# Score products of an attention block: three passes over both groups, or two passes for each group on stacked query halves

## The chip, the cores and the metric

The kernel runs on one core of a Trainium2 chip. The metric is the device time of one execution in microseconds. Its engines are TensorE (PE in the profile, PEld for its weight loads), VectorE (DVE), ScalarE (ACT), GpSimd (POOL) and SyncE (SP), which issues the DMAs. They run side by side and wait for one another through semaphores.

## What is computed

One layer of a hybrid decoder on 1024 new positions (the prompt) and 8 single decode steps: an input projection, sliding-window attention and a gated linear recurrence side by side, an output projection, and a gated feed-forward layer, all in fp32. The change touches the attention of the prompt alone:

```
s = einsum('bnqhgd,bnkhd->bnhgqk', qb, kk) * HEAD_DIM ** -0.5   # window 128, 2 key/value heads
p = sink softmax over the masked s
o = einsum('bnhgqk,bnkhd->bqhgd' by block, p, vv)
```

There are 8 query heads of 64 dimensions and 2 key/value heads (groups). A block is 128 queries; it sees 256 keys, its own block and the one before (the first block sees 128).

## The kernel before

**Precision.** A product of fp32 matrices is made on TensorE from operands of the type fp32r. Each operand is split in a high part (a copy rounded to fp32r) and a low part (the difference), and three products are summed: high with high, high with low, low with high.

**Layout.** Activations lie with features on the 128 partitions. A query tile `mix[:, t]` holds head t of group 0 on partitions 0 to 63 and head t of group 1 on partitions 64 to 127. The keys `kraw` lie in the same way. The tiles `k_hi` and `k_lo` (128 x 2 x 1032) have a section for each group: in section g only the partitions of group g hold keys, the others are zero (memsets of POOL, lines 972 to 975). So one product with 128 partitions and both sections as moving operand (512 columns) gives the scores of both groups, and the zeros keep the groups apart.

**Order of the work.** The input projection is cut into units: 22 weight tiles by three chunks of 344 columns, 24 products each (line 1482, called by line 1529). A list ORDER gives their order; a unit has two ticks of 12 products. Every other step is hung on a tick, and each engine walks the ticks in order. The first four weight tiles (keys, values, the recurrence's input, query tile 0) run chunk by chunk, while the input's third chunk is still being loaded and split.

**Key steps.** When the keys' unit of chunk c is done and rotated (function `rope`, lines 1929 to 1933), ScalarE makes the high part of each group (lines 1174 to 1177) and VectorE the low part (`keys_low`, lines 1935 to 1941), which signals `k_low`. On VectorE's queue then follow the read of the next unit (line 1970), the reciprocal and diagonal tiles `diag` of the row norms (line 1882), for which TensorE waits at line 1513, and at chunk 1 the low part of the input's third chunk (line 1871), for which TensorE waits at line 1482.

**Attention items.** An item is one query tile and one block: 4 x 8 = 32 items, the first at tick 16, one every two ticks. Its steps are Q (ScalarE copies the queries' high part `q_hi`, line 1198; VectorE subtracts for `q_lo`, line 2044), S (TensorE's scores, lines 1557 to 1559; VectorE adds the mask and takes the maxima, line 2051; ScalarE's exponentials, line 1204), PT (transposes of the probabilities, line 1566), PV (product with the values, line 1575; scaling, line 2066) and OT (transpose back, line 1580). TensorE waits in S for `k_low`, for `q_low` of the item and for the maxima of the item before. From tick 54 on the recurrence runs beside it: for each of 4 heads a preparation on VectorE (lines 2076, 2077), a product of diagonals (line 1596) and seven levels (TensorE line 1611, VectorE lines 2013, 2014 and 2099). The loop over items ends before the second half of the recurrence; output projection and feed-forward (lines 1753, 1793) follow.

In the profile both `q_hi` and weight tiles copied by ScalarE carry line 1068, that of the helper `copy`.

Of the kernel before, what the change touches and what calls it, by code (L numbers as in the profile page):

```python
# [14 lines left out]
P = 128  # L15
# [191 lines left out]
def build(nc, t_in, t_out):  # L207
# [99 lines left out]
    q_hi, oo = at("q_hi", [P, 2, P], F32R, at_mix + 5 * 4 * ROWS)  # L307
    q_lo, _ = at("q_lo", [P, 2, P], F32R, oo)
# [386 lines left out]

    V_GROUPS = [(0, 4), (4, 4), (8, 1)]
# [272 lines left out]
    def _(pool):  # L969
        pool.memset(cos[:], 1.0).then_inc(sem("pool_set"), 1)  # L970
        pool.memset(sin[:], 0.0).then_inc(sem("pool_set"), 1)
        pool.memset(k_hi[:].bitcast(F32), 0.0).then_inc(sem("pool_set"), 1)
# [93 lines left out]
    def _(act):  # L1066
# [86 lines left out]
        for tick in range(TICKS):  # L1153
# [14 lines left out]
            for step in rot_steps(tick):  # L1168
                if step[0] == "k_high":
                    c = step[1]  # L1170
                    act.wait_ge(sem("rope"), ROPE_UNITS.index(unit_index("k", 0, c)) + 1)
                    if c == 0:
                        act.wait_ge(sem("pool_set"), 3)
                    for g in range(NKV):
                        h = slice(HD * g, HD * g + HD)
                        ins = copy(k_hi[h, g, cols(c)], kraw[h, cols(c)])
                    ins.then_inc(sem("k_high"), 1)
# [12 lines left out]
            for step, i in attention_steps(tick):  # L1190
                t, j, e = i // NBLK, i % NBLK, i % 2
                k0 = WIN if j == 0 else 0
                if step == "Q":
# [4 lines left out]
                    copy(q_hi[:, e, :], mix[:, t, P * j:P * j + P]).then_inc(sem("q_high"), 1)  # L1198
# [19 lines left out]
            for step in recurrence_steps(tick):  # L1218
                h = step[1]
                if step[0] in ("ita", "itb"):  # L1220
# [4 lines left out]
                    if h == 0 and not a:  # L1225
                        act.wait_ge(sem("pool_set"), 4 + CH)
# [248 lines left out]
    def _(pe):  # L1475
# [42 lines left out]
        for tick in range(TICKS):  # L1518
# [28 lines left out]
            for step, i in attention_steps(tick):  # L1547
                t, j, e = i // NBLK, i % NBLK, i % 2
                kbs = (1,) if j == 0 else (0, 1)
                if step == "S":  # L1550
# [6 lines left out]
                    for n, (a, b) in enumerate(((q_hi, k_hi), (q_hi, k_lo), (q_lo, k_hi))):  # L1557
                        mm = pe.matmul(out[:, :, k0:], a[:, e, :], b[:, :, P * (j - 1) + k0:P * (j + 1)], start=(n == 0), stop=(n == 2))
# [292 lines left out]
    def _(dve):  # L1851
# [83 lines left out]
        def keys_low(c):  # L1935
            dve.wait_ge(sem("k_high"), c + 1)
            dve.wait_ge(sem("pool_set"), 4 + c)
            for g in range(NKV):
                h = slice(HD * g, HD * g + HD)
                ins = dve.tensor_tensor(k_lo[h, g, cols(c)], kraw[h, cols(c)], k_hi[h, g, cols(c)].bitcast(F32), ALU.subtract)  # L1940
            ins.then_inc(sem("k_low"), 1)
# [82 lines left out]
        for tick in range(TICKS):  # L2024
# [14 lines left out]
            for step, i in attention_steps(tick):  # L2039
                t, j, e = i // NBLK, i % NBLK, i % 2  # L2040
                k0 = WIN if j == 0 else 0
                if step == "Q":
                    dve.wait_ge(sem("q_high"), i + 1)
                    dve.tensor_tensor(q_lo[:, e, :], mix[:, t, P * j:P * j + P], q_hi[:, e, :].bitcast(F32), ALU.subtract)\
                        .then_inc(sem("q_low"), 1)
# [24 lines left out]
            for step in recurrence_steps(tick):  # L2070
# [18 lines left out]
                if step[0] == "level":  # L2089
                    n = step[2]  # L2090
                    dve.wait_ge(sem("level_mm"), LEVELS * h + n + 1)
                    if n == 0 and h == 0:
                        dve.wait_ge(sem("pool_set"), 4 + CH)
# [38 lines left out]
            for step in sample_steps(tick):  # L2132
                n = DECB * NQ
                if step[0] == "ks_t":

                    dve.wait_ge(sem("pool_set"), 5 + CH)
# [426 lines left out]
```

## Time and profile before

| | |
|---|---|
| median of 3 runs | 1258.96 us (1256.0 to 1259.29) |
| the profiled execution | 1255.75 us, span 1253.9 us |
| mean granted clock of TensorE | 0.989 |
| TensorE busy | 1210.5 us, 97% of the span |
| VectorE busy | 894.9 us, 71% |
| ScalarE busy | 469.2 us, 37% |
| GpSimd busy | 235.1 us, 19% |
| chain that ended last | 58% on TensorE, 6% on VectorE, 1% waiting for nothing shown |

The span is the time between the first and the last instruction of the profiled execution; the time of the execution itself includes what lies around it. The page's busiest groups are the feed-forward's products (line 1753, about 200 us for each of the first three forms); those of the input projection (line 1482) come to 519 us of overlapping matmul time. In a timeline a matmul's length includes its latency, so what TensorE pays for one is the distance to the start of the next.

### The profile page before, as it was taken

How to read it: one execution, taken by the hardware profiler on the slowest of the kernel's cores; microseconds unless marked ns; L12 is line 12 of the kernel's file. 1: busy time of each engine (PE TensorE's matmuls, PEld its weight loads, DVE VectorE, ACT ScalarE, POOL GpSimd, SP SyncE). 2: the span in 40 equal slices, each digit the busy share in tenths (PEclk: the TensorE clock that was granted, in tenths of full speed). 3: DMA queues.
4: the chain of work that ended last, by engine and by line, in shares of the span. 5: the costliest groups of instructions: out<-in, count | busy, mean ns of one | idle time of the engine just before them, and what ended most of it. 6: DMA issues, size and time to landing. Idle time of an engine off the chain costs nothing.

```text
span 1253.9 us, 23628 instructions
## 1 busy us (share of the span) xinstructions
PE 1210.5 (97%) x9421; PEld 1186.6 (95%) x9421; DVE 894.9 (71%) x1535; ACT 469.2 (37%) x969; POOL 235.1 (19%) x166
## 2 busy tenths in 40 slices
PE   9799999999998999999999999999999999999995
PEld 8789999999997899998999999999999999999995
DVE  4767667575757666689977788889887565567674
ACT  5544433523121155445422232222223235455541
POOL 1000010010102000000023336567664220000013
PEclk9999999999999899999999999999999999999998
DMA  8411110103011323424254456677666376675557
GB/s 288 114 50 59 33 35 1 37 18 87 18 53 51 84 82 124 124 80 127 78 158 154 144 180 225 211 249 229 220 219 221 127 218 208 197 255 186 152 122 107
DMA packets 168237, 167.00 MB, mean 133 GB/s; under 512 B 18904, under 2 KB 121064, under 8 KB 167600
## 3 DMA queue, kind: packets, MB, share of 16 engines
q1 hardware_dynamic: 164864, 161.26, 41.7%
q0 software_dynamic: 3264, 4.23, 2.3%
q8 instruction: 75, 1.23, 0.4%
q14 instruction: 34, 0.28, 0.1%
HBM read 113.92 MB, written 52.57 MB: 133 GB/s over the span
## 4 chain that ended last, share of the span: by engine, by line
PE 58%; DVE 6%; issue 1%; ACT 1%; POOL 0%; POOLq 0%; DVEq 0%; ACTq 0%
PE pair L1753 32%; PE pair L1793 17%; PE pair L1712 6%; PE pair L1482 1%; DVE mix L2248 1%; DVE mix L2273 1%; PE pair L1611 1%; DVE w_lo L2206 1%; DVE qinv L2244 1%; PE pair L1678 0%; PE pair L1695 0%; DVE mix L2468 0%; DVE act_lo L2256 0%; POOL y_cols_out L1049 0%; DVE act_hi L2462 0%
## 5 line engine op out<-in xcount | busy, mean ns | idle before, releaser
L1753 PE MATMUL pair<-act_hi,w_hi 128*128 128x258 f32 x704 | 199.6, 284 | 4.2 <-DVE w_lo L2206 2.7
L1753 PE MATMUL pair<-act_hi,w_lo 128*128 128x258 f32 x704 | 198.9, 283 | 0.0
L1753 PE MATMUL pair<-act_lo,w_hi 128*128 128x258 f32 x704 | 198.7, 282 | 0.0
L1793 PE MATMUL pair<-a_ring,w_hi 128*128 128x258 f32 x1056 | 189.6, 282 | 0.6 <-DVE mix L2411 0.5
L1482 PE MATMUL pair<-act_hi,w_hi 128*128 128x344 f32 x528 | 178.7, 338 | 5.9 <-DVE act_lo L1871 4.3
L1482 PE MATMUL pair<-act_hi,w_lo 128*128 128x344 f32 x528 | 170.2, 322 | 0.0
L1482 PE MATMUL pair<-act_lo,w_hi 128*128 128x344 f32 x528 | 170.0, 322 | 0.0
L1793 PEld LDWEIGHTS pair<-a_ring,w_hi 128*128 128x128 f32 x1056 | 162.4, 189 | 1.6 <-DVE mix L2411 0.9
L1753 PE MATMUL pair<-s_hi,w_lo 128*128 128x258 f32 x528 | 149.3, 283 | 0.0
L1753 PE MATMUL pair<-s_hi,w_hi 128*128 128x258 f32 x528 | 149.2, 283 | 0.0
L1753 PE MATMUL pair<-mix_r,w_hi 128*128 128x258 f32 x528 | 149.0, 282 | 0.0
L1793 PE MATMUL pair<-a_ring,w_lo 128*128 128x258 f32 x528 | 148.2, 281 | 0.0
L1068 ACT ACTIVATE w_hi<-rawx 128x512 fp32r<-128x512 f32 (+1 forms) x95 | 67.6, 712 | 192.8 <-PE pair L1753 79.7
L1753 PEld LDWEIGHTS pair<-act_hi,w_hi 128*128 128x128 f32 x704 | 133.1, 189 | 5.0 <-DVE w_lo L2206 3.1
L1753 PEld LDWEIGHTS pair<-act_lo,w_hi 128*128 128x128 f32 x704 | 132.9, 189 | 0.1
L1753 PEld LDWEIGHTS pair<-act_hi,w_lo 128*128 128x128 f32 x704 | 132.7, 188 | 0.0
L1482 PEld LDWEIGHTS pair<-act_hi,w_hi 128*128 128x128 f32 x528 | 100.8, 191 | 12.4 <-issue 9.2
L1482 PEld LDWEIGHTS pair<-act_lo,w_hi 128*128 128x128 f32 x528 | 100.9, 191 | 0.8
L1482 PEld LDWEIGHTS pair<-act_hi,w_lo 128*128 128x128 f32 x528 | 100.5, 190 | 0.0
L1793 PEld LDWEIGHTS pair<-a_ring,w_lo 128*128 128x128 f32 x528 | 100.0, 189 | 0.0
L1753 PEld LDWEIGHTS pair<-mix_r,w_hi 128*128 128x128 f32 x528 | 99.9, 189 | 0.0
L1753 PEld LDWEIGHTS pair<-s_hi,w_hi 128*128 128x128 f32 x528 | 99.7, 189 | 0.0
(318 smaller groups left out, 2645.7 us busy)
## 6 DMA issues: line engine op xcount, KB each, us to landing
raw<-w_up_dram SPq DMA_DIRECT2D x26, 512.0 KB, 5.2
a_in<-h_sums SPq DMA_DIRECT2D x44, 258.0 KB, 3.3
rawx<-w_gate_dram SPq DMA_DIRECT2D x22, 512.0 KB, 5.1
w_quarter<-w_down_dram SPq DMA_DIRECT2D x44, 256.0 KB, 3.9
w_sums<-w_quarter SPq DMA_DIRECT2D x44, 256.0 KB, 4.6
rawx<-w_sums SPq DMA_DIRECT2D x44, 256.0 KB, 3.9
raw<-w_in_dram SPq DMA_DIRECT2D x18, 512.0 KB, 4.2
h_scratch<-mix SPq DMA_DIRECT2D x23, 258.0 KB, 2.0
```

The source lines that it names most:

```text
L1068: return act.activation(out, in_, ACT.Copy)
L1482: mm = pe.matmul(out, a[:, k, :], b[:, k, cols(c)], start=(k == 0 and s == 0), stop=(k == KT - 1 and s == 2))
L1611: mm = pe.matmul(BL[n % 2][0:P - hs, P // 2 * c:P // 2 * (c + 1)], hk[:, P * c:P * c + P - hs], qv[:, c, :, 1, :], start=True, stop=True)
L1712: mm = pe.matmul(bank[(slot + 2) % 4][:, 0:QW], a[:, k, :], b[:, k, quad(slot // NOUT)], start=(k == 0 and s == 0), stop=(k == KT - 1 and ...
L1753: mm = pe.matmul(pair[psum_pair(n)][:, s, 0:QW], a[:, r, half + k, :], b, start=(k == 0 and i == 0), stop=(k == 3 and i == 2))
L1793: mm = pe.matmul(dpair(mt)[:, s, 0:QW], b[:, cut], a, start=(m == 0 and n == 0), stop=(m == HALVES - 1 and n == 2))
L2206: dve.tensor_tensor(w_lo[:, r, 0:k], src, w_hi[:, r, 0:k].bitcast(F32), ALU.subtract).then_inc(sem("wf_split"), 1)
L2244: then(dve.reciprocal(qinv[:], qinv[:]))
L2248: ins = dve.scalar_tensor_tensor(out=x, in0=x, scalar=gain[:, PRE_FFN, k:k + 1], in1=qinv[:], op0=ALU.mult, op1=ALU.mult)
L2273: dve.tensor_tensor(dst, x, y, op).then_inc(sem("s_sum"), 1)
```

## The change

The tiles `q_hi` and `q_lo` are replaced by `q_both`, with a section for each group. In section g the partitions of group g hold the high part of that group's queries, and the other half of the partitions holds the low part of the same queries. `k_hi` gets the high keys of group g on both halves of the partitions (so its memset goes), while `k_lo` keeps its zeros. One product of section g with `k_hi` then sums high with high and low with high; one with `k_lo` adds high with low. Each group needs two products of its own 256 columns (128 in the first block). ScalarE's copy for Q and VectorE's subtraction for Q become two half-width instructions each, and `keys_low` gets two more half-width copies for each chunk.

```diff
-    q_hi, oo = at("q_hi", [P, 2, P], F32R, at_mix + 5 * 4 * ROWS)
-    q_lo, _ = at("q_lo", [P, 2, P], F32R, oo)
+    q_both, _ = at("q_both", [P, 2, NKV, P], F32R, at_mix + 5 * 4 * ROWS)
...
+    def half(g, other=False):
+
+        h = 1 - g if other else g
+        return slice(HD * h, HD * h + HD)
...
-        pool.memset(k_hi[:].bitcast(F32), 0.0).then_inc(sem("pool_set"), 1)
...
-                    if c == 0:
-                        act.wait_ge(sem("pool_set"), 3)
                     for g in range(NKV):
-                        h = slice(HD * g, HD * g + HD)
-                        ins = copy(k_hi[h, g, cols(c)], kraw[h, cols(c)])
+                        ins = copy(k_hi[half(g), g, cols(c)], kraw[half(g), cols(c)])
                     ins.then_inc(sem("k_high"), 1)
...
-                    copy(q_hi[:, e, :], mix[:, t, P * j:P * j + P]).then_inc(sem("q_high"), 1)
+                    for g in range(NKV):
+                        ins = copy(q_both[half(g), e, g, :], mix[half(g), t, P * j:P * j + P])
+                    ins.then_inc(sem("q_high"), 1)
...
-                    for n, (a, b) in enumerate(((q_hi, k_hi), (q_hi, k_lo), (q_lo, k_hi))):
-                        mm = pe.matmul(out[:, :, k0:], a[:, e, :], b[:, :, P * (j - 1) + k0:P * (j + 1)], start=(n == 0), stop=(n == 2))
+                    for g in range(NKV):
+                        for n, k in enumerate((k_hi, k_lo)):
+                            mm = pe.matmul(out[:, g, k0:], q_both[:, e, g, :], k[:, g, P * (j - 1) + k0:P * (j + 1)],
+                                           start=(n == 0), stop=(n == 1))
                     mm.then_inc(sem("at_s"), 1)
...
-            dve.wait_ge(sem("pool_set"), 4 + c)
+            dve.wait_ge(sem("pool_set"), 3 + c)
             for g in range(NKV):
-                h = slice(HD * g, HD * g + HD)
-                ins = dve.tensor_tensor(k_lo[h, g, cols(c)], kraw[h, cols(c)], k_hi[h, g, cols(c)].bitcast(F32), ALU.subtract)
+                dve.tensor_tensor(k_lo[half(g), g, cols(c)], kraw[half(g), cols(c)], k_hi[half(g), g, cols(c)].bitcast(F32), ALU.subtract)
+            for g in range(NKV):
+                ins = dve.tensor_copy(k_hi[half(g, True), g, cols(c)], k_hi[half(g), g, cols(c)].bitcast(F32))
             ins.then_inc(sem("k_low"), 1)
...
-                    dve.tensor_tensor(q_lo[:, e, :], mix[:, t, P * j:P * j + P], q_hi[:, e, :].bitcast(F32), ALU.subtract)\
-                        .then_inc(sem("q_low"), 1)
+                    for g in range(NKV):
+                        ins = dve.tensor_tensor(q_both[half(g, True), e, g, :], mix[half(g), t, P * j:P * j + P],
+                                                q_both[half(g), e, g, :].bitcast(F32), ALU.subtract)
+                    ins.then_inc(sem("q_low"), 1)
```

The other edits are three more waits on `pool_set` whose number falls by one, since one memset is gone.

## Rows read from the trace of the kernel before

**Rows 1.** Busy time of each engine in two stretches of the attention (us, busy, count).
```profile
52.00:76.00 24.00, 19.25 (x120) 17.72 (x119) 18.14 (x65) 8.72 (x28) 1.60 (x2) 0.97 0.10 23
76.00:176.00 100.00, 98.52 (x673) 95.86 (x672) 64.42 (x240) 46.43 (x155) 3.06 (x3) 1.00 0.14 44
```

**Rows 2.** Timeline of TensorE: start, length, instruction, count; one full item's score step.
```profile
146.34 0.60 PE L1566 MATMUL pair<-ident,prob 128*128 128x128 f32 x4
146.78 0.27 PE L1580 MATMUL pair<-ident,orow 128*128 128x128 f32 x1
146.80 0.48 PE L1558 MATMUL pair<-k_hi,q_hi 128*128 128x512 f32 x1
147.12 0.39 PE L1558 MATMUL pair<-k_lo,q_hi 128*128 128x512 f32 x1
...
147.59 0.33 PE L1482 MATMUL pair<-act_hi,w_hi 128*128 128x344 f32 x1
```

**Rows 3.** Timeline of TensorE: the score step of a block 0.
```profile
152.71 0.36 PE L1558 MATMUL pair<-k_hi,q_hi 128*128 128x256 f32 x1
152.91 0.28 PE L1558 MATMUL pair<-k_lo,q_hi 128*128 128x256 f32 x1
...
153.15 0.32 PE L1482 MATMUL pair<-act_hi,w_hi 128*128 128x344 f32 x1
```

**Rows 4.** Timelines of VectorE and TensorE, 35 to 50 us; in brackets the wait before.
```profile
35.38 1.04 DVE L1940 TENSOR_TENSOR k_lo<-r_f,k_hi 64x344 fp32r<-64x344 f32 x2 [1.15 <-ACT k_hi L1068]
36.44 0.52 DVE L1970 TENSOR_TENSOR r_i<-pair,r 128x344 f32<-128x344 f32 x1
...
37.81 0.94 PE L1513 MATMUL pair<-diag,ones 128*128 128x128 f32 x6 [1.46 <-DVE diag L1882]
...
47.56 1.04 DVE L1940 TENSOR_TENSOR k_lo<-r_f,k_hi 64x344 fp32r<-64x344 f32 x2 [4.33 <-ACT k_hi L1068]
...
49.78 0.59 PE L1482 MATMUL pair<-act_hi,w_hi 128*128 128x344 f32 x1 [3.49 <-DVE act_lo L1871]
```

**Rows 5.** Timelines of VectorE, ScalarE and TensorE, 55 to 76 us: the first items.
```profile
55.13 0.36 PE L1558 MATMUL pair<-k_hi,q_hi 128*128 128x256 f32 x1 [1.68 <-DVE q_lo L2044]
...
61.71 0.29 DVE L2044 TENSOR_TENSOR q_lo<-mix,q_hi 128x128 fp32r<-128x128 f32 x1
...
62.10 0.47 PE L1558 MATMUL pair<-k_hi,q_hi 128*128 128x512 f32 x1 [0.99 <-issue]
...
67.88 0.29 DVE L2044 TENSOR_TENSOR q_lo<-mix,q_hi 128x128 fp32r<-128x128 f32 x1 [2.20 <-ACT q_hi L1068]
...
73.60 0.29 DVE L2044 TENSOR_TENSOR q_lo<-mix,q_hi 128x128 fp32r<-128x128 f32 x1 [1.12 <-ACT q_hi L1068]
...
75.51 0.66 PE L1539 MATMUL pair<-ident,r_q 128*128 128x128 f32 x4 [1.62 <-DVE r_i L1970]
```

**Rows 6.** Groups of instructions by line: count, busy us, mean ns of one, wait before.
```profile
L1983 DVE TENSOR_SCALAR r_f<-th,lbt 128x344 f32<-128x344 f32 x12 | 5.5, 456 | 3.3 <-ACT th L1140 3.3
L2044 DVE TENSOR_TENSOR q_lo<-mix,q_hi 128x128 fp32r<-128x128 f32 x32 | 9.6, 300 | 12.2 <-ACT q_hi L1068 11.9
```

**Rows 7.** Timelines of VectorE and TensorE: a tight item in the paced stretch.
```profile
156.54 0.29 DVE L2044 TENSOR_TENSOR q_lo<-mix,q_hi 128x128 fp32r<-128x128 f32 x1
156.75 1.22 DVE L1866 TENSOR_TENSOR w_lo<-raw,w_hi 128x1024 fp32r<-128x1024 f32 x1
...
158.08 0.48 PE L1558 MATMUL pair<-k_hi,q_hi 128*128 128x512 f32 x1
```

**Rows 8.** Waits of VectorE, 75 to 290 us: total us, times, longest.
```profile
DVE hq L2013 <- PE pair L1611: 6.5, 6, 1.2
```

**Rows 9.** A stretch (granted clock 0.50), then two pieces of the chain that ended last.
```profile
404.80:415.00 10.20, 10.20 (x34) 7.54 (x32) 4.80 (x9) 1.44 (x2) 0.00 (x0) 0.50 0.18 51
...
409.61 3.74 PE pair L1482 x12
...
415.74 1.95 PE pair L1482 x12
```

More of the change, by code:

```diff
@@ L1225, in _ @@
                     if h == 0 and not a:
-                        act.wait_ge(sem("pool_set"), 4 + CH)
+                        act.wait_ge(sem("pool_set"), 3 + CH)
                     copy(irow[:, 4 * a:4 * a + 4, :], BR.rearrange("p (b d) -> p b d", b=4)).then_inc(sem("i_rows"), 1)
@@ L2092, in _ @@
                     if n == 0 and h == 0:
-                        dve.wait_ge(sem("pool_set"), 4 + CH)
+                        dve.wait_ge(sem("pool_set"), 3 + CH)
                     decay(h, n)
@@ L2134, in _ @@
                 if step[0] == "ks_t":
-                    dve.wait_ge(sem("pool_set"), 5 + CH)
+                    dve.wait_ge(sem("pool_set"), 4 + CH)
                     dve.wait_ge(sem("at_out"), NITEM)
```

## The prediction, made before the changed kernel was run

> **What bounds the kernel now.** The profile's page comes first: TensorE is busy 97% of the span, the chain that ended last lies on it almost alone, and the attention is a small stage of a long kernel. So the question is what TensorE's time is made of where the change works. The table of stretches [rows 1] shows two regimes. From 76 to 176 us TensorE is busy 98.5 of 100 us with VectorE at 64.4: TensorE paces. From 52 to 76 us TensorE is busy 19.25 of 24 us, VectorE 18.14: here TensorE waits, and VectorE paces. The timeline of one item's score step gives what TensorE pays per item [rows 2, 3]; the timelines of the start [rows 4, 5] give what VectorE and ScalarE pay and who waits for them. The reader should see that this change takes from the first account and adds to the second.
>
> **What TensorE saves.** A group's score step was three passes of 512 columns for both key/value groups; now it is four of 256 columns, two for each. It runs 32 times, four of them (block 0 of each query tile) with half the columns. For 512 columns it holds TensorE from 146.80 to 147.59, 0.79 us: 0.32 for the first pass, which waits and refills, 0.47 for the two others [rows 2]. What 256 columns cost stands in the block-0 step: first pass 0.20 (152.71 to 152.91), the next two together 0.24 (152.91 to 153.15), each with its own weight load, 0.44 in all [rows 3]. Four such passes: 0.20 + 3 x 0.12 = 0.56. **Saving 0.23 us an item.** In block 0 the new passes have 128 columns, which no row shows in this format. Nearest is the transposes' 128 columns: four between 146.34 and 146.78, 0.11 each [rows 2]. Taken: 0.20 + 3 x 0.11 = 0.53 against 0.44, +0.09. From below, not under the 0.44 of today, since a fourth weight load is added; from above, a narrow pass as dear as a wide one, 4 x 0.23 + 0.09 = 1.01, +0.57.
>
> **What VectorE and ScalarE pay.** (a) Key chunks: each of the three gets two more copies of 64 x 344 on VectorE, ahead of the signal for the low keys. Nearest in size and in having one input is the TENSOR_SCALAR of 344 elements, 0.456 us [rows 6]. Work on half of the partitions does not overlap with its neighbour: the two low-key subtractions and the start of what follows are 35.38 and 36.44, 0.53 each [rows 4], while a full-width operation lets the next start 0.21 after its own start though it lasts 0.29 (156.54, 156.75 in [rows 7]). So 0.48 a copy, **0.96 a chunk**; bounds 0.30 and 0.53 a copy. The lower end has a page behind it. The Trainium skill (VectorE: DVE Perf Modes, The perf-mode tier table) has a copy of fp32 within SBUF run at two elements a cycle; by it a copy would take about 0.3 us (estimate) and the sum below would fall by 0.7 us. The 0.456 of the one-input row speaks against it, so the row decides. (b) Queries: one full-width copy on ScalarE and one full-width subtraction on VectorE per item become two half-width ones. With 0.29 us each [rows 5, 6] and no overlap, the pair needs 0.62 on VectorE where 0.21 was needed, **+0.41**, and its result is 0.30 later; on ScalarE **+0.30**. Bounds: +0.20 on either if halves do overlap, +0.5 if the operation behind is held too. (c) Off POOL goes the memset of the high keys, and off ScalarE the wait for it. POOL does it at the very start, long before the first high keys (VectorE gets those at 35.38 in [rows 4]), and the loads of the rotation tables wait only for the two memsets ahead of it: 0. The semaphore counts only move by one.
>
> **Where (a) and (b) lie.** In the start they are on the path, step by step.
> - Chunk 0: behind the low keys on VectorE stand a read of a product, the reciprocal and the diagonal tiles; TensorE idles 1.46 us for those at 37.81 [rows 4]. ScalarE's row copy, its third part of the input and the next high keys hang on TensorE's answer, so the whole chain shifts: **+0.96**.
> - Chunk 1: VectorE had waited 4.33 us for these high keys, and behind them stands the low part of the input, for which TensorE idles 3.49 us at 49.78 [rows 4]. **+0.96**.
> - Chunk 2: the copies stand before a 1.12 us wait of VectorE for the query's high part (73.60 in [rows 5]). They fit in it, so 0; without it, 0.96.
> - Items 0 and 1: TensorE idles 1.68 us for item 0's low part and 0.99 us before item 1 [rows 5], whose low part is ready at 61.71 + 0.29. VectorE's order carries each pair to the next maxima: **2 x 0.41**.
> - Items 2 and 3: exponentials, ScalarE's copy, then VectorE's subtraction follow one another, VectorE waiting 2.20 and 1.12 us for ScalarE [rows 5]. Both additions count: **2 x 0.71**. At 75.51 TensorE has its last such wait, 1.62 us, for a read behind item 3's low part.
> Sum at 75.5 us: 0.96 + 0.96 + 0.82 + 1.42 = **+4.2 us**. TensorE's savings on items 0 to 2 fall into these waits and count nothing.
>
> From item 3 on TensorE paces. Items 3 to 31 are 26 full and 3 of block 0: 26 x 0.23 - 3 x 0.09 = **-5.7 us**. There (b) costs nothing as long as its cover holds. In a tight item the low part is finished at 156.83 and used at 158.08 [rows 7], 1.25 us of slack against 0.30 + 0.30 = 0.60 later. In the recurrence levels VectorE still waits 6.5 us in six places for TensorE's level products [rows 8], against 0.41 each item. If that cover were gone, 0.41 would be paid per item. What is late next, once scores are shorter, is nothing: TensorE goes on with its own products.
>
> **Sum: +4.2 - 5.7 = -1.5 us**, against the profiled execution's own 1255.75 us (span 1253.9), so 1254.2; that execution lies 3.2 us under the median of the three runs, 1258.96, so on the median 1257.5. Bounds of the unknown prices: copies at 0.30 (-0.7) and halves that overlap (-1.0) give -3.2; copies at 0.53 (+0.2), block 0 at 1.01 (3 x 0.48 = +1.4) and some of the covers short (+0.4) give +0.5. About 0.3%, 3.8 us, is what a measurement of this kernel can tell from no change.
>
> **Rivals.**
> - *The start is cheap* (10%). Both lower bounds hold, and chunk 1's copies hide as well, because TensorE takes the low parts of the input one by one and could catch up on them. Then the start costs 0.60 for chunk 0 and 4 x 0.20 for the pairs, 1.4 instead of 4.2: 1.4 - 5.7 = -4.3, median 1254.7. For it: only the chunks' rows show halves that do not overlap. Against it: the waits at 37.81 and 49.78 are plain, and something is added ahead of each.
> - *The clock* (14%). TensorE runs at 0.50 of its clock (1.2 instead of 2.4 GHz) from 404.8 to 415 us, after short waits in the recurrence; twelve products that need 1.95 us take 3.74 there [rows 9]. So 10.2 x (1 - 1.95 / 3.74) = 4.9 us hang on when these waits fall, and the change shifts them. If the stretch stays at 2.4 GHz: -1.5 - 4.9 = -6.4, median 1252.6. It can as well grow. The change does nothing to those waits themselves, so the forecast leaves it as it is.
> - *VectorE and ScalarE become the pace of the attention* (14%), the case on the slow side. Place: the wait for the query's low part, and VectorE's turn between two level products. Price: 0.41 in every item from 4 on, 28 x 0.41 = 11.5, so up to +10, median 1269; if only the twelve items beside the recurrence pay, 12 x 0.41 = 4.9, so +3.4, and with the 0.60 of the query chain in some of them +4 to +7, median 1263 to 1266. It decides once VectorE's waits for TensorE in that stretch [rows 8] are used up. Against: VectorE is busy only 64.4 of 100 us [rows 1] and has these waits.
> - *It does not save columns' time* (2%): if a 256-column pass after a weight load costs as much as a 512-column one, the step would be 1.01 instead of 0.79, and items 3 to 31 would cost 26 x 0.22 + 3 x 0.57 = 7.4 instead of saving: +11.6, median 1270.5. [rows 3] speak against it directly.
>
> **How the numbers follow.** The forecast has 60%: 1257.5, its own range 1255.8 to 1259.5. Within 0.3% is that case alone: 0.60. Faster: 0.10 + 0.14 = 0.24. Slower: 0.14 + 0.02 = 0.16. The range goes down to 1252.5, over the cheap start and most of the clock case, and up to 1262, to the edge of the slow case; left out are most of that case and the last one.
>
> **What would show it.** Right: the score step shows four passes of 256 columns, 0.56 us from its first to the next product; the wait for the diagonal tiles grows from 1.46 to some 2.4 us, the one at 49.78 from 3.49 to 4.4; TensorE's last wait of the start ends near 79.7 instead of 75.51; the level products and everything after come about 1.5 us earlier than before. Wrong: half-width subtractions whose next operation starts 0.2 us after them; copies of 0.3 us; new waits of TensorE for the low queries or for VectorE's level step between 80 and 290 us; another stretch at half clock, or one fewer.

## The result and the profile after: a little slower, and the loss lies where no loss was predicted

The changed kernel takes 1268.38 us in the median of 8 runs (1261.6 to 1271.21), the kernel before 1258.54 us beside it (8 runs, 1254.63 to 1259.34). The ratio is 1.0084, with a 95% interval of 1.0067 to 1.0100: about 10 us slower, where 1.5 us faster was forecast and the range ended at 1262. The profiled execution of the changed kernel took 1271.21 us, the slowest of its eight, so its trace holds 15.5 us more than the trace of before where the medians differ by 9.8. One execution of one kernel below (scores alone, round opened) took 2357.28 us, in a slow state, and is left out of its ratio.

The page of after, busy time of each engine:
```profile
PE 1216.2 (96%) x9453; PEld 1192.8 (94%) x9453; DVE 913.1 (72%) x1573; ACT 479.0 (38%) x1001; POOL 234.2 (18%) x165
```
The windows of after; the columns are those of [rows 1]. The second window is moved by the 4 us that the attention starts later:
```profile
52.00:76.00 24.00, 20.30 (x119) 19.29 (x118) 18.70 (x65) 8.33 (x29) 1.60 (x2) 0.88 0.09 19
80.00:180.00 100.00, 94.00 (x656) 90.59 (x657) 65.73 (x246) 47.55 (x161) 0.00 (x0) 1.00 0.14 44
```
In the stretch where TensorE was busy 98.52 of 100 us and was said to pace, it is now busy 94.00, at full clock, although each item asks less of it. The waits of TensorE in that window say where:
```profile
PE pair L1561 <- issue: 4.8, 7, 1.0
PE pair L1541 <- DVE r_i L1975: 2.7, 1, 2.7
PE pair L1570 <- ACT esk L1208: 0.7, 2, 0.5
```
The second line is no real part of it: it is the last wait of the start, which ends at 79.89. The first is new: seven waits before score steps (line 1561). Before, from 76 to 176 us, TensorE had one wait in all, 1.5 us for the recurrence.

The view starts a wait only when the last product's latency is over, so it tells less than is lost. The distance of the starts tells more. The timeline of TensorE in after, item 6:
```profile
98.66 0.27 PE L1584 MATMUL pair<-ident,orow 128*128 128x128 f32 x1
99.35 0.36 PE L1561 MATMUL pair<-k_hi,q_both 128*128 128x256 f32 x1 [0.42 <-issue]
```
0.69 us lie between these two where 0.02 lie in [rows 2] (146.78 to 146.80). The nine such distances from item 6 to item 14 sum to 7.35 us. Summed in this way from item 5 to item 15, TensorE starts 7.0 us later than in before in front of the scores, 1.3 in front of the transposes (PT) and 0.5 in front of the product with the values (PV), and its ten score steps are 2.0 us shorter: 6.8 us lost in all.

**The two steps that were costed.** TensorE in after, a full item's score step:
```profile
151.67 0.35 PE L1561 MATMUL pair<-k_hi,q_both 128*128 128x256 f32 x1 [0.96 <-issue]
151.87 0.28 PE L1561 MATMUL pair<-k_lo,q_both 128*128 128x256 f32 x1
...
152.22 0.32 PE L1484 MATMUL pair<-act_hi,w_hi 128*128 128x344 f32 x1
```
From 151.67 to 152.22 are 0.55 us, where [rows 2] have 0.79 and 0.56 was predicted. The block-0 step of after:
```profile
112.23 0.30 PE L1561 MATMUL pair<-k_hi,q_both 128*128 128x128 f32 x1 [0.97 <-issue]
...
112.70 0.37 PE L1484 MATMUL pair<-act_hi,w_hi 128*128 128x344 f32 x1
```
It takes 0.47 us, 0.03 more than [rows 3]; +0.09 was predicted. Now the start, on VectorE and TensorE, against [rows 4, 5]:
```profile
35.70 1.04 DVE L1943 TENSOR_TENSOR k_lo<-r_f,k_hi 64x344 fp32r<-64x344 f32 x2 [1.15 <-ACT k_hi L1071]
...
36.74 0.68 DVE L1945 CAST k_hi<-k_hi 64x344 fp32r<-64x344 f32 x2
37.46 0.52 DVE L1975 TENSOR_TENSOR r_i<-pair,r 128x344 f32<-128x344 f32 x1
...
38.83 0.94 PE L1515 MATMUL pair<-diag,ones 128*128 128x128 f32 x6 [2.16 <-DVE diag L1886]
...
51.48 0.62 PE L1484 MATMUL pair<-act_hi,w_hi 128*128 128x344 f32 x1 [4.18 <-DVE act_lo L1875]
...
57.25 0.30 PE L1561 MATMUL pair<-k_hi,q_both 128*128 128x128 f32 x1 [2.31 <-DVE q_both L2050]
...
79.89 0.66 PE L1541 MATMUL pair<-ident,r_q 128*128 128x128 f32 x4 [2.72 <-DVE r_i L1975]
```
The waits grew where they were said to, though less: 1.46 to 2.16 and 3.49 to 4.18, some 0.7 us each where 0.96 was predicted. The last wait of the start ends at 79.89 instead of 75.51, 4.38 us later where 4.2 were predicted. The two copies of a chunk take 0.72 us together (36.74 to 37.46), not 0.96.

**The account.** The start of the same product in both timelines, item by item, shows where after falls behind. "Item 5" is the first product of item 5's score step, the last row the first product after the attention and the recurrence (line 1712 of before, 258 columns).

| point | before, us | after, later by |
|---|---|---|
| item 3 | 76.5 | 4.38 |
| item 5 | 88.6 | 3.95 |
| item 10 | 117.2 | 7.64 |
| item 15 | 146.8 | 11.10 |
| item 19 | 169.9 | 10.51 |
| item 31 | 275.3 | 10.40 |
| first 258-column product | 466.0 | 14.87 |

Ten items, from 5 to 15, lose 7.15 us, 0.71 each. From item 15 to item 31 after gains 0.70 on before, though it has one stretch at half clock more than before there, at 262.6. Behind item 31 it loses 4.5 us, in three more such stretches. The windows of these four (PEclk is the figure behind POOL's); before has none of them:
```profile
262.60:266.00 3.40, 3.40 (x16) 3.40 (x16) 1.57 (x3) 0.00 (x0) 0.89 (x4) 0.51 0.00 0
348.00:351.40 3.40, 3.40 (x16) 3.40 (x15) 1.40 (x4) 1.44 (x2) 0.00 (x0) 0.50 0.02 5
433.30:436.70 3.40, 3.40 (x21) 3.03 (x20) 2.26 (x4) 0.49 (x1) 0.00 (x0) 0.50 0.81 215
447.00:450.40 3.40, 3.40 (x13) 3.40 (x13) 2.77 (x6) 1.44 (x2) 0.00 (x0) 0.50 0.36 108
```
By the ratio of [rows 9], such a stretch costs 3.4 x (1 - 1.95 / 3.74) = 1.6 us. So the three behind item 31 make, by this estimate, 4.9 of the 15.5 us in this trace. That is near the 5.7 us by which the trace exceeds the difference of the medians; whether the executions near the median lack them, no run shows. The start of after has one such stretch more than before as well, near 58 us. The 7.15 us of items 5 to 15 are the loss to explain.

### The profile page after: what moved, and what is told of

The parts are those of the page before. It is cut to its first block, busy times and chain, and to the rows that moved or that the text cites. A ratio compares the mean times of both kernels' runs of the same rounds, so it can differ in the third digit from the quotient of the medians.

```text
span 1269.4 us, 23760 instructions
## 1 busy us (share of the span) xinstructions
PE 1216.2 (96%) x9453; PEld 1192.8 (94%) x9453; DVE 913.1 (72%) x1573; ACT 479.0 (38%) x1001; POOL 234.2 (18%) x165
## 4 chain that ended last, share of the span: by engine, by line
PE 51%; DVE 10%; issue 3%; ACT 2%; POOL 0%; POOLq 0%; DVEq 0%; ACTq 0%
PE pair L1757 26%; PE pair L1797 17%; PE pair L1716 5%; PE pair L1484 1%; ACT w_hi L1071 1%; DVE mix L2255 1%; DVE w_lo L2213 1%; PE pair L1615 1%; DVE mix L2280 1%; DVE qinv L2251 1%; DVE t L2223 0%; DVE u_tmp L2358 0%; DVE v L2358 0%; PE pair L1682 0%; DVE t L2222 0%
## 5 line engine op out<-in xcount | busy, mean ns | idle before, releaser
L1484 PE MATMUL pair<-act_hi,w_hi 128*128 128x344 f32 x528 | 181.5, 344 | 6.5 <-DVE act_lo L1875 4.6
L1484 PE MATMUL pair<-act_hi,w_lo 128*128 128x344 f32 x528 | 173.0, 328 | 0.0
L1484 PE MATMUL pair<-act_lo,w_hi 128*128 128x344 f32 x528 | 172.8, 327 | 0.0
```

The lines of the kernel that those rows point to most:

```text
L1484: mm = pe.matmul(out, a[:, k, :], b[:, k, cols(c)], start=(k == 0 and s == 0), stop=(k == KT - 1 and s == 2))
```

## The experiments

The expectations speak of three theories. **A**: the loss is a closed round over VectorE and ScalarE: row maxima of item i, exponentials of i, query copy of i + 1, query subtraction of i + 1, and behind it on VectorE's queue the weight and rotation work and the maxima of i + 1. TensorE is not in it, so it is not shortened by shorter scores, and 0.30 + 0.41 = 0.71 us of half-width work is paid in full. **B**: the stretches at half clock make it. **C**: each half-width pair costs its 0.41 everywhere.

### First set: the parts of the change alone, and the round opened

**Key copies alone.** The kernel before, with two further copies of each chunk on VectorE:
```diff
+            for g in range(NKV):
+                h = slice(HD * g, HD * g + HD)
+                ins = dve.tensor_copy(k_hi[h, g, cols(c)], k_hi[h, g, cols(c)].bitcast(F32))
```


> The kernel before, with only the two extra half-width copies of each key chunk put in on VectorE (each copies a section onto itself). Theory A (the loss is a closed round: the maxima of item i, its exponentials, the queries' copy and subtraction for item i+1 follow one another on VectorE and ScalarE, whose queues run them in this order, and the halved query steps made that round longer than TensorE's 5.7 to 5.9 us an item): only the start is touched, 0.7 us for each of chunks 0 and 1, so +1.4 us on the kernel before, waits between 80 and 175 us as before. Theory B (the loss comes from the start and from TensorE falling to half clock in other stretches because the start shifted): +6 us or more, with more stretches at 0.50.

Measured: 1258.51 against 1257.1, ratio 1.0013 [1.0001, 1.0025]. The score steps of items 3 to 19 begin 0.84 to 0.87 us later, a constant, where 1.4 was expected. Nothing else comes of the keys.

**Query halves alone.** The kernel before, old scores, with the copy and the subtraction in halves:
```diff
-                    copy(q_hi[:, e, :], mix[:, t, P * j:P * j + P]).then_inc(sem("q_high"), 1)
+                    for g in range(NKV):
+                        h = slice(HD * g, HD * g + HD)
+                        ins = copy(q_hi[h, e, :], mix[h, t, P * j:P * j + P])
+                    ins.then_inc(sem("q_high"), 1)
...
+                        ins = dve.tensor_tensor(q_lo[h, e, :], mix[h, t, P * j:P * j + P], q_hi[h, e, :].bitcast(F32), ALU.subtract)
```


> The kernel before, with only the queries' copy (ScalarE) and subtraction (VectorE) cut into two half-width ones; the three 512-column passes stay. Theory A: the start costs 2.2 us, and TensorE gets new waits before the score step in the items with key or query units beside them (80 to 155 us), 5 to 8 us in all; +7 to +10 us. Since TensorE's own item is 0.23 us longer than in the changed kernel, a little less waiting than there. Theory B: about +2 us and no new waits after 80 us. Theory C (each half-width pair taxes its neighbours by 0.41 us in all items): +11 us, spread evenly, in the recurrence stretch too.

Measured: 1268.71 against 1257.1, ratio 1.0092 [1.0077, 1.0106], +11.6 us, more than the 7 to 10 expected of A: item 3 is 4.90 us late where 2.2 was expected. This alone is as slow as the whole change. It is 5.40 us late at item 5, 12.34 at item 15, and 12.64 at item 31. That flat stretch behind item 15 refutes C: there are 16 more items there, each with the same two pairs, and they cost nothing. TensorE's waits from 80 to 180 us:
```profile
PE pair L1561 <- issue: 3.9, 7, 0.8
PE pair L1542 <- DVE r_i L1973: 2.5, 1, 2.5
```
These are waits before the scores of the same seven items as in after (6, 8 to 12 and 14), so they do not come from the new scores.

**Scores alone.** The kernel before, with four passes of 256 columns; the product of high queries and low keys is left out:
```diff
+                    for g in range(NKV):
+                        for n, (a, b) in enumerate(((q_hi, k_hi), (q_lo, k_hi))):
+                            mm = pe.matmul(out[:, g, k0:], a[:, e, :], b[:, g, P * (j - 1) + k0:P * (j + 1)],
+                                           start=(n == 0), stop=(n == 1))
```


> The kernel before, with only the score step replaced by four passes of 256 columns (high queries and low queries with the high keys, for each group); the product of high queries with low keys is left out, so that VectorE's and ScalarE's work stays as it was. Theory A and C: TensorE's saving alone, 26 x 0.23 - 3 x 0.09 = 5.7 us, and no cost: -4 to -6 us. Theory B: -6 us give or take stretches at half clock, 1.7 us each. If instead the narrow passes cost TensorE more than the distances between starts say, about 0 or more.

Measured: 1256.93 against 1257.1, ratio 0.9992 [0.9976, 1.0009], where 4 to 6 us less were expected. The saving that the prediction had from item 3 on is not there: from item 3 to item 16 this kernel gains 0.35 us on before, 0.03 an item instead of 0.23. It comes only where the recurrence runs: from item 16 to item 31 it gains 2.8. Where did 2.6 us of TensorE's time go, with nothing added to any other engine? The trace answers with the maxima. Timeline of VectorE in this kernel, the last step of the maxima of two items in a row:
```profile
119.98 0.16 DVE L2059 TENSOR_TENSOR tsum<-sink,negm 128x2 f32<-128x2 f32 x1
...
127.28 0.16 DVE L2059 TENSOR_TENSOR tsum<-sink,negm 128x2 f32<-128x2 f32 x1
```
The kernel before:
```profile
119.78 0.16 DVE L2057 TENSOR_TENSOR tsum<-sink,negm 128x2 f32<-128x2 f32 x1
...
126.07 0.42 DVE L2051 CUSTOM_DVE_ANT_0 sm<-pair,amask 128x256 f32<-128x256 f32 x1
...
127.08 0.16 DVE L2057 TENSOR_TENSOR tsum<-sink,negm 128x2 f32<-128x2 f32 x1
```
Both take 7.30 us for this round, whatever the scores cost, and from item 4 to item 14 the ten rounds take 58.5 us here and 58.7 in before. On TensorE the saving turns into waiting: from item 5 to item 15 its score steps are 2.0 us shorter, and it starts 0.4 us later in front of the scores, 0.6 in front of PT and 0.3 in front of PV. And the maxima at 126.07 waited for nothing: the scores lay ready. For all maxima of before from 88 to 144 us, the view of that tile says:
```profile
L2051 DVE CUSTOM_DVE_ANT_0 sm<-pair,amask x20: 286/420/425, 90.9 to 142.6; 128x256 f32<-128x256 f32 x18, 128x128 f32<-128x128 f32 x2
its engine sat idle before it (us, times) until:
  PE pair L1558: 0.3, 1
```
Twenty instructions, ten items, and 0.3 us of waiting for TensorE. So already in before TensorE delivered ahead and VectorE took when it came round. In after and in the kernel with the scores alone, the same view shows no wait for TensorE at all.

**The round opened.** The changed kernel with the step Q one tick earlier for every item, ahead of the maxima of the item before on both queues:
```diff
-            for step, i in (("PT", d // 2 - 1), ("OT", d // 2 - 2), ("S", d // 2)):
+            for step, i in (("Q", d // 2 + 1), ("PT", d // 2 - 1), ("OT", d // 2 - 2), ("S", d // 2)):
...
-            for step, i in (("PV", (d - 3) // 2), ("Q", (d + 1) // 2)):
+            for step, i in (("PV", (d - 3) // 2),):
```


> The changed kernel, with the queries' step of item i+1 moved one tick earlier on ScalarE and VectorE, ahead of the maxima and exponentials of item i, so that it no longer follows them; the same instructions otherwise. Theory A: the round is open, the waits of TensorE before the score step between 80 and 155 us go (6.5 us by the profile, with the exponentials' 0.7), and most of the query pairs' part of the start: 8 to 11 us less than the changed kernel, about as the kernel before or up to 2 us faster. Theory C: the same work on the same engines, so no change, +10 us on the kernel before. Theory B: at most 2 us better than the changed kernel.

Measured: 1261.93 against 1257.1, ratio 1.0036 [1.0022, 1.005]. That is 6.5 us under the changed kernel's median, or 5.0 if each is held against the runs of before beside it, less than the 8 to 11 expected. In the place in question the loss is gone: 4.49 us late at item 5, 3.67 at item 15, a gain of 0.8 where after lost 7.15 (the shorter scores could give about 2.0), and from 80 to 175 us TensorE waits once, 0.5 us. The rest is elsewhere: from item 20 to item 31 it loses 3.6 us, and behind item 31 another 3.0. Waits of TensorE from 180 to 290 us, first in this kernel, then in before:
```profile
PE pair L1615 <- DVE hk L2019: 2.3, 4, 0.6
PE pair L1600 <- DVE hk L2084: 2.1, 1, 2.1
```
```profile
PE pair L1596 <- DVE hk L2077: 1.5, 1, 1.5
```
The first line is new. Beside the recurrence, the early query step stands ahead of VectorE's work on the levels.

### Second set: the earlier step only up to item 16

In these kernels the early step of the diff above has a condition, which is the line shown, and on the odd ticks the same items are passed over.

**Scores alone, round opened.** The third kernel of the first set with
```diff
+                if 0 <= i < NITEM and (step != "Q" or i <= 16):
```


> The kernel with only the score step changed (four passes of 256 columns, the product of high queries with low keys left out, query steps full width as before), and now the query steps of items up to 16 one tick earlier, ahead of the maxima and exponentials of the item before. Theory A: already in the kernel before, the round over VectorE and ScalarE is as long as TensorE's item between items 4 and 15, so the score step's saving there was lost in e3_scores; with the round open it appears. Between the scores of items 4 and 16 the shift against the kernel before falls by about 2.6 us (11 x 0.23), where e3_scores fell by 0.9; 3 to 5 us less than the kernel before in all. Rival (narrow passes give nothing beside key and query units for a reason on TensorE): as e3_scores.

Measured: 1252.95 against 1257.41, ratio 0.9962 [0.9946, 0.9978], about 4.5 us less, in the expected range. Now the items from 3 to 16 gain 2.57 us on before, where they gained 0.35; the expected figure was 2.6. The view of the maxima, from 88 to 140 us:
```profile
L2055 DVE CUSTOM_DVE_ANT_0 sm<-pair,amask x20: 287/422/425, 89.3 to 139.6; 128x256 f32<-128x256 f32 x18, 128x128 f32<-128x128 f32 x2
its engine sat idle before it (us, times) until:
  PE pair L1561: 1.5, 5
```
In five of ten items VectorE waits for the scores: TensorE paces again, and a shorter TensorE step counts.

**The whole change, round opened, key copies on ScalarE.** These copies read `kraw`, behind the high keys, and have a semaphore of their own:
```diff
+                    for g in range(NKV):
+                        ins = copy(k_hi[half(g, True), g, cols(c)], kraw[half(g), cols(c)])
+                    ins.then_inc(sem("k_both"), 1)
```


> The changed kernel, with the query steps of items up to 16 one tick earlier and the key chunks' two extra copies made by ScalarE (which idles there) straight from the rotated keys, instead of by VectorE. Theory A: the round is open; the start costs 1.4 us less than in the changed kernel, the levels of the recurrence have no new waits as in e4_early. Shift of the scores of item 5 about +3 us, of the last level step about 0 to +1; -1 to +2 us on the kernel before. Theory B (shifted half-clock stretches decide): anything beyond +4.

Measured: 1259.07 against 1257.41, ratio 1.0016 [1.0001, 1.003]. Item 0 starts only 0.24 us late instead of 2.12, but item 3 is 3.55 late: the copies no longer delay item 0, and the pairs of items 0 to 3 stay. At item 5 it is 4.16 late where about 3 was expected. Its start also holds 13.7 us at half clock, and this was not separated from the pairs.

**The whole change with POOL's help.** POOL makes the key copies and, for group 1, the query's copy and subtraction; each of its instructions waits for the one before, and its copy of the mask `lmask` moves to tick 22:
```diff
+                    mark(pool.tensor_copy(q_both[half(g), e, g, :], mix[half(g), t, P * j:P * j + P]), "q_phi")
+                    after()
+                    mark(pool.tensor_tensor(q_both[half(g, True), e, g, :], mix[half(g), t, P * j:P * j + P],
+                                            q_both[half(g), e, g, :].bitcast(F32), ALU.subtract), "q_plow")
```


> The changed kernel, with GpSimd, idle in this stage, making the key chunks' extra copies and the query copy and subtraction of group 1; ScalarE and VectorE each keep one half-width query instruction (0.29 us) for the one full-width one of before, order unchanged. Theory A: the round on VectorE and ScalarE is as long as before the change, so items 4 to 15 keep TensorE's old pace (shift flat, 0 to +1), the start costs under 1 us, and items 16 to 31 save 0.23 us each: -2 to -3 us on the kernel before. If GpSimd's two instructions (0.4 us each by its 128-element rows, more if it is slower at fp32r) come late: waits of TensorE before the score step.

Measured: 1259.32 against 1257.41, ratio 1.0026 [1.001, 1.0042], so +1.9 where a gain was expected. The start is nearly free (item 3 0.89 late, item 5 0.44), but items 5 to 15 lose 2.92, 0.29 each. With one half left on each engine the round should have been as long as in before. The timeline of VectorE and POOL in one item:
```profile
131.38 0.28 DVE L2096 TENSOR_TENSOR q_both<-mix,q_both 64x128 fp32r<-64x128 f32 x1 [1.24 <-ACT q_both L1116]
131.70 0.52 DVE L1980 TENSOR_TENSOR mix<-pair,cos 128x344 f32<-128x344 f32 x1
...
133.47 0.63 POOL L1024 TENSOR_TENSOR q_both<-mix,q_both 64x128 fp32r<-64x128 f32 x1
133.71 0.42 DVE L2113 TENSOR_TENSOR den<-den,esk 128x2 f32<-128x2 f32 x1
134.16 0.17 DVE L2114 RECIPROCAL rden<-den 128x2 f32<-128x2 f32 x1
```
The next operation starts 0.32 us behind the one half-width subtraction, where 0.21 lie behind a full-width one [rows 7]; and an addition of two elements, 0.15 us long at 118.38 in before, takes 0.42 while POOL's subtraction runs and pushes the next one from 0.19 to 0.45 us behind it. In seven of the ten rounds this addition takes 0.36 to 0.42 us, each time beside POOL's subtraction, and 0.15 in the three where it does not meet it. Together 0.37 us, and the round here (129.77 to 135.37, the last step of the maxima) is 5.60 where the same one in before is 5.23.

**The same, round opened up to item 16** by the line
```diff
+                if 0 <= i < NITEM and (step != "Q" or i <= 16):
```

> f3_pool with the query steps of items up to 16 one tick earlier as well. Theory A: the saving of items 4 to 15 comes too: -4 to -5.5 us on the kernel before, the best of all. Rival (the added work costs wherever it lies): no better than e4_early, +4 us.

Measured: 1255.46 against 1257.41, ratio 0.9988 [0.9978, 0.9999]. That is less than the 4 to 5.5 us expected, but it is the best version of the whole change: item 5 is 1.49 late, item 15 is 0.36 early, item 31 is 1.5 early. It beats before by 1.5 us in the estimate, at the edge of what can be told from nothing.

### Third set: is it the round, or only an earlier step that is good by itself?

**The kernel before, round opened** by the same line, with nothing else changed:
```diff
+                if 0 <= i < NITEM and (step != "Q" or i <= 16):
```

> The kernel before, with only the query steps of items up to 16 moved one tick earlier. Theory A: the round is as long as TensorE's item there but not longer, TensorE never waits, so opening it alone gives nothing: within 1 us of the kernel before, and the scores of items 4 to 16 at the same distances. If it is 3 us or more faster, the gain of f1_scores_early over e3_scores came from the move itself and not from the open round.

Measured: 1256.7 against 1255.85, ratio 1.0006 [0.9992, 1.0019]; from item 3 to item 31 every item comes 0.27 to 0.37 us before its old place, a constant. The maxima now wait for the scores in six of the ten items from 88 to 144 us, 2.9 us in all, so here TensorE paces, and at the old speed: opening the round is worth nothing where the round and TensorE's item are equally long.

**Query halves alone, round opened**: the second kernel of the first set with
```diff
+                if 0 <= i < NITEM and (step != "Q" or i <= 16):
```

> e2_halves (the kernel before with its query steps in halves) with the query steps of items up to 16 one tick earlier. Theory A: the same instructions as e2_halves, but the shift no longer grows between the scores of items 5 and 15 (there 6.9 us); 7 to 9 us less than e2_halves, +2 to +4 on the kernel before. Theory C (each pair taxes its engine's neighbours wherever it lies): as e2_halves, +11.

Measured: 1261.85 against 1255.85, ratio 1.004 [1.0024, 1.0055]: 6.0 us over before, where the same halves in the closed round cost 11.6; +2 to +4 was expected. Item 5 is 2.92 late and item 16 is 2.99 late: eleven items with two pairs each cost 0.07 us together, and TensorE has no wait at all from 80 to 175 us. With the first kernel of this set it settles the place of the loss. What is left of the 6.0 us lies in the start and behind item 31 (from 1.68 late to 6.24).

**POOL's help, opened for items 5 to 16 only**, to keep the early step out of the start:
```diff
+                if 0 <= i < NITEM and (step != "Q" or 5 <= i <= 16):
```

> f4_pool_early, with the earlier tick only for items 5 to 16, so that the first items keep the old order. The start as in f3_pool (shift of item 4's scores +0.7 instead of +1.7), then the falling shift of f4_pool_early: -2 to -3 us on the kernel before, about 1 us better than f4_pool_early, if the start's order is what cost there.

Measured: 1257.57 against 1255.85, ratio 1.0013 [1.0, 1.0025]: a miss. Item 4 is 3.51 us late where 0.7 was expected. It is not the order of the steps, which up to item 4 is that of the kernel with POOL's help and a closed round, where item 4 is 0.65 late. Item 0 even starts a little earlier here than there (55.66 us), though TensorE waits longer before it, having finished its products sooner. The line of item 0 and the window behind it:
```profile
55.33 0.45 PE L1610 MATMUL pair<-k_hi,q_both 128*128 128x128 f32 x1 [3.14 <-POOL q_both L1026]
55.40:62.20 6.80, 6.80 (x27) 6.49 (x28) 3.64 (x18) 1.22 (x7) 1.29 (x4) 0.52 0.00 0
```
Here TensorE runs at half clock for 6.8 us in which it has work: from the first product behind item 0's scores to the transposes of its probabilities take 7.83 us (56.22 to 64.05), in the other kernel 5.22 (56.13 to 61.35), where a stretch of 3.4 us lay before item 0. So the same instructions, with the half-clock stretch elsewhere, put item 1 at 64.18 instead of 62.65, and a second stretch that only this trace has, 3.4 us from 79 us on, delays item 4. The question of the start's order stays open.

## Why the prediction was wrong

**The round, read from the rows.** Timeline of VectorE in after, from one item's last maxima step to the next:
```profile
128.14 0.16 DVE L2064 TENSOR_TENSOR tsum<-sink,negm 128x2 f32<-128x2 f32 x1
...
131.03 0.59 DVE L2050 TENSOR_TENSOR q_both<-mix,q_both 64x128 fp32r<-64x128 f32 x2 [2.44 <-ACT q_both L1071]
131.65 1.23 DVE L1870 TENSOR_TENSOR w_lo<-raw,w_hi 128x1024 fp32r<-128x1024 f32 x1
132.79 0.51 DVE L1933 TENSOR_TENSOR mix<-pair,cos 128x344 f32<-128x344 f32 x1
...
134.79 0.15 DVE L2067 TENSOR_TENSOR den<-den,esk 128x2 f32<-128x2 f32 x1
...
135.18 0.42 DVE L2058 CUSTOM_DVE_ANT_0 sm<-pair,amask 128x256 f32<-128x256 f32 x1
...
136.19 0.16 DVE L2064 TENSOR_TENSOR tsum<-sink,negm 128x2 f32<-128x2 f32 x1
```
and of ScalarE in the gap:
```profile
128.34 0.51 ACT L1206 ACTIVATE prob<-sm,negm 128x256 f32<-128x256 f32 x1 [3.26 <-DVE tsum L2064]
...
129.43 1.05 ACT L1071 ACTIVATE w_hi<-raw 128x1024 fp32r<-128x1024 f32 x1
130.39 0.61 ACT L1071 ACTIVATE q_both<-mix 64x128 fp32r<-64x128 f32 x2
```
Each step begins where the one before it lets it: 0.20 to the exponentials, 1.09 to the weight copy, 0.96 to the query's copy, 0.64 to the subtraction, 0.62 to the low weights, 1.14 to the rotation, 2.00 to the denominator, 0.39 to the maxima, 1.01 to their last step: 8.05 us with no TensorE in it. The same round of before, from 119.78 to 127.08, has 0.32 and 0.21 in the place of 0.64 and 0.62, and is 7.30 long. The other rounds are shorter, most because they lack the weight copy and the low weights. From item 4 to item 14 the ten rounds take 58.7 us in before (84.57 to 143.25) and 65.9 in after (88.69 to 154.57); TensorE's ten items from 5 to 15 take 58.2 us in before and 65.3 in after. That rounds and items agree proves nothing, since each hands over to the other once an item. What tells is who waits at the hand-over. In before almost nobody does: the maxima wait 0.3 us in ten items, and each score step from item 3 to item 16 starts 0.02 to 0.08 us behind the product in front. So TensorE's item and the round were equally long. In after the maxima wait for nothing and TensorE waits. So what is added to the round is paid, and what TensorE saves is not seen.

**Point by point.**
- *TensorE's price of the scores*: right, 0.55 us for 0.56. Block 0: 0.03 for 0.09.
- *Prices of the halves*: right where it mattered. The pair on VectorE holds what follows for 0.62 us as predicted, the pair on ScalarE 0.61 to 0.64. The term for the key copies was too large, 0.72 for 0.96 a chunk. The row taken for it, a TENSOR_SCALAR of 344 elements at 0.456, was a poor guide: the group of these copies has 334 ns as the mean of one. The Trainium skill (VectorE: DVE Perf Modes, The perf-mode tier table), with two elements a cycle for a copy of fp32 within SBUF, had led to an estimate of about 0.3 us, and the trace agrees.
- *The start*: right in its sum, +4.38 for +4.2, not in its parts. The key copies alone cost 0.85 there instead of 1.92, the query halves alone 4.90 at item 3 instead of 2.24, and the parts do not add up to the whole. In the trace with the halves alone the half-clock stretch of the start is 10.2 us long instead of 3.4. How much of the 4.90 that makes was not separated: the kernel with the scores alone has a stretch as long in its start and is 0.11 late at item 3, while two kernels with the same instructions up to item 4 (POOL's help, with and without the early step from item 5) stand 2.86 us apart at item 4. So a start is not told from one trace to better than a few us, and the good sum is partly luck.
- *The step that failed*: "There (b) costs nothing as long as its cover holds. In a tight item the low part is finished at 156.83 and used at 158.08 [rows 7], 1.25 us of slack". That is item 17, for whose predecessor VectorE's maxima wait 1.74 us for TensorE: there TensorE paces. It was taken for the slack of every item. The timeline line of that wait, and the row of all such waits of the maxima from 75 to 290 us (total, times, longest), both of before:
```profile
153.44 0.29 DVE L2051 CUSTOM_DVE_ANT_0 sm<-pair,amask 128x128 f32<-128x128 f32 x1 [1.74 <-PE pair L1558]
DVE sm L2051 <- PE pair L1558: 18.7, 16, 2.3
```
Of these 18.7 us only 0.3 lie between 88 and 144 us. Where the maxima wait for nothing there is none to give, and a slack at one hand-over is used up by the second or third item if each round is longer than TensorE's item; what counts is the length of the round. The new waits before score steps, 0.42 at 99.35 and 0.96 at 151.67, are where it ran out.
- *"Items 3 to 31 are 26 full and 3 of block 0: ... -5.7 us"* failed by the same step. Some 12 of the items, 4 to 15, lie where the round is as long as TensorE's item, and there the saving was not to be had even without the halves: 0.35 instead of 2.6 us. Behind item 16 it came.
- *The rival* of VectorE and ScalarE as the pace (14%) was what happened, and its end of the scale, 1269, is near the 1268.4 measured, but not by its working. Its place was the items from 4 on in general with 0.41 each; the runs show items 5 to 15 with 0.71 each. Beside the recurrence, where its deciding point was put, VectorE's waits for the level products fell from 6.5 us [rows 8] to 3.4 in after and were not used up, and almost nothing is paid. The argument against it, VectorE busy 64.4 of 100 us, is no argument: VectorE and ScalarE wait for each other in turn, and each is idle for the other's part.
- *The clock*: an item in its own right in this trace, near 5 us behind item 31, with more short stretches than before. What sets where they fall was not tried by itself; what they cost is in the table below. They come and go with every kernel here: a stretch at 176 us in before is missing with the two key copies, and item 20 then comes 0.73 us early where item 19 was 0.87 late.
- *The other two rivals* did not come: the start was not cheap (4.38 us), and a score step of four narrow passes takes 0.55 us, not 1.01.

The part from item 31 to the first 258-column product, in all the traces, against before:

| time at half clock in it, us | kernels | longer than before by, us |
|---|---|---|
| 10.2, as in before | key copies alone; halves alone; scores alone, opened; before, opened; POOL's help; POOL's help, opened | -0.3 to 0.1 |
| 13.6 | scores alone | 1.1 |
| 17.0 | round opened for every item; POOL's help, opened from item 5 | 3.0, 3.2 |
| 20.4 | after; halves alone, opened; key copies on ScalarE | 4.5, 4.6, 4.5 |

So what after loses behind item 31 goes with its half-clock time.

**What is shown and what is not.** Shown: the loss from item 5 to 15 comes from the query halves (they alone bring it), needs the closed round (with the round opened it is 0.07 us), and the round hides TensorE's saving (0.35 against 2.57). So A explains this part. B holds behind item 31, where the comparison of traces alone shows that the loss follows the time at half clock. C is refuted. Not shown: what brings those stretches about, how much of the start's 4.38 us they make, and so how the last few of the 10 us divide.

## What to carry to other kernels

Before a small addition on an engine with idle time is costed at nothing, look at who waits at the hand-over to the busy engine. If the consumer never waits for the engine at "97%" (here 20 maxima with 0.3 us of wait), the round through the other engines is at least as long as the busy engine's own work, and it has to be added up, from one maxima step to the next, with the work queued in between. If it must grow, open it first: put the next item's preparation ahead of the current item's reductions in program order, and only where nothing more urgent is behind it. Half-width instructions on two halves of the partitions are two instructions in series, not one shared.

## What the runs showed of the hardware

- Half-width instructions do not overlap with a neighbour on the other half. Two subtractions of 64x128 on VectorE hold it for 0.62 us where one of 128x128 holds it 0.21 until the next starts. On ScalarE the subtraction that waits for the pair of copies starts 0.64 us behind the first, and 0.32 behind one full-width copy. For VectorE the Trainium skill has the rule (VectorE: DVE Perf Modes, Two Vector instructions with no wait between them): an instruction whose input or output begins in another quarter of the partitions than the last one's starts only when all before it are finished. The rows agree.
- A copy from fp32 to fp32r within SBUF, 64x344, takes 334 ns on VectorE, where the subtraction of the same size takes 511.
- Beside a subtraction on POOL, an addition of two elements on VectorE took 0.42 instead of 0.15 us, and POOL's own subtraction 0.64 instead of 0.46, in six of the seven rounds in which they met (in the seventh 0.36 and 0.46).
- In fp32r four passes of 128 columns with a weight load each take 0.47 us and four of 256 take 0.55: half the columns save 15%.
- Time at half clock is paid where TensorE has work: with 10.2 us more of it than in before, the part from item 31 to the first 258-column product took 4.5 to 4.6 us longer, in three kernels.
